# A hybrid attention and delta-rule block: gating and weight-tile work put in another order

## The chip, the cores and the metric

The kernel runs on one NeuronCore of a Trainium2 chip. The metric is the device time of one execution in microseconds (us), the median of several. The engines are TensorE (PE in the profile; PEld is its weight load), VectorE (DVE), ScalarE (ACT), GpSimd (POOL) and SyncE (SP, which here only issues DMA transfers and waits). They run side by side and meet at semaphores.

## The reference

One layer over a sequence of 1024 rows and 1024 channels, float32:

```python
mod = silu(c) @ ada_w + ada_b                     # shift, scale, gate
h = rms_norm(x, norm_g) * (1 + scale) + shift
p = h @ w_in                                      # 1024 x 6152, cut into twelve parts
o_sb = stick_breaking_attention(rms_norm(sb_q), rms_norm(sb_k), sb_v) * silu(sb_z)
q, k, v = split(silu(causal_conv4(dn_q | dn_k | dn_v)))
o_dn = gated_delta_rule(l2(q), l2(k), v, sigmoid(dn_b), decay(dn_a))
o_dn = rms_norm(o_dn, dn_norm_g) * silu(dn_z)
y = sigmoid(merge_sb) * (o_sb @ w_branch_sb) + sigmoid(merge_dn) * (o_dn @ w_branch_dn)
out = x + gate * (y @ w_out)
```

## The kernel before

Every large product is made in three passes: both operands are split into a high part (a cast) and a low part (the rest), and TensorE adds high x high, high x low and low x high in one PSUM bank. `project` (L839) does this for a tile of 128 output channels, one half of 512 rows at a time: 8 blocks of 128 inputs x 3 matmuls, 24 for a half tile.

**Weight tiles.** The list `tiles` holds, in order: tiles 0 and 1 of the gate columns (z of the attention), tiles 2 to 13 of the delta channels (T3 = 2), tiles 14 to 35 (the other z tiles and the two merge gates; T4 = 14), tiles 36 to 43 of the branch stage (T6 = 36), half from `w_branch_sb` and half from `w_branch_dn`. There is one raw buffer, `w3raw`, and two split ones, `w3hl`. For each tile `load_w3` (L815) waits until the low half of the tile before is written, then issues the DMA; `split_hi` (L821, VectorE) casts it, once TensorE has used the tile before the last; `split_lo` (L828, GpSimd) writes the low half; TensorE waits for both in `have_w3`. From the delta stage on the loads are issued by ScalarE (`copy_z`, piece 11 of 16 of a tile), the cast at piece 3 and the low half at piece 4 (`next_hi`, `next_lo`).

**The z pieces.** 24 tiles of z and merge gates don't belong to a stage: they fill TensorE where other work leaves it idle. One piece is one block of 128 inputs (3 matmuls), 16 are a tile, 8 a half tile. `z_piece` issues it into one of two banks; ScalarE copies a finished half tile (L923) and stores it to `z_scratch` (L887). TensorE may begin half tile m only when half tile m - 2 is copied.

**The order of the work**, written out by hand on each engine:

- `*_0`, `*_1`: norm, modulation, projection of q, k, v.
- `*_2`: attention in 64 steps (n = 0 to 63) and a few after. On TensorE each step has scores (L1054, L1056), `fill_2` (z pieces by the table `fill_at`), products with the values (L1085) and transposes of the weights (L1068); ScalarE makes sigmoids (L1132), copies transposed weights (L1140), the filled half (L914) and the outputs (L1149); VectorE scans (L1184). Split tile 1 lies in a buffer of its own; the second slot of `w3hl` lies under the attention's scan buffer `stick`.
- `*_3`: the twelve delta channels: projection, ScalarE's copy (L1283), four taps of the convolution on VectorE (L1303, L1306), silu. `dve_3` begins with `split_hi(T3 + 1)`, then the small decay chain `decays_in`, with help of ScalarE; before the second channel it casts tile 4.
- `*_4`: the delta rule over eight row blocks, with z pieces in between: `back_to_rows` (L1388), inverses, then a scan of eight steps (`from_state`, `solved`, `to_state`, `to_output`), `normalize_out` on VectorE and 32 closing transposes, `turn_output` (L1528), four to a block, which ScalarE copies (`copy_out_t`, L1661). The last z pieces ahead of these are those of half tile 41. SP's `sp_4` counts half tiles: in each turn m it waits for the copy of half tile m.
- `*_5`: the six half tiles 42 to 47 that are left (`left`) and the gates of eight tiles i, 0 to 3 from the attention, 4 to 7 from the delta rule: `silu_z` (L1914, ScalarE), `gated` (L1933, L1935, VectorE), `high_part` (L1918, ScalarE), `low_part` (L1940, VectorE). SP loads z and the attention's output for them in `load_gating` (L1904, L1906), two tiles a step, step 0 behind the end of `*_4` on all engines. The steps after those load the first half of `w_out` (L1909).
- `*_6`: the branch stage, eight tiles, two halves each. TensorE makes both branch products; ScalarE the sigmoid of the merge gates in `sg` (L1996); VectorE multiplies (L2015), GpSimd adds (L2034), VectorE casts the sum (`high`, L2005), GpSimd makes its low part (`low`, L2025). `high` and `low` of half n - 1 stand behind the product and the sum of half n. `split_w7` (L2045, L2047), the split of the first half of `w_out`, stands in this loop at n = 2 and 4. SP's `sp_6` issues the load of tile 37, then waits for all z stores, then loads `sg` (L1973).
- `*_7`: the output projection (L270 to L272), gate and residual.

Between the stages 1, 2 and 3 every engine but TensorE waits for the others (`end_phase`).

## Time and profile before

| what | us |
|---|---|
| median of 3 runs | 972.64 (972.01 to 973.81) |
| the profiled execution, its own time | 973.91 |
| its span, first to last instruction | 971.9 |
| TensorE busy / weight load | 939.9 / 789.2 |
| VectorE busy | 531.8 |
| ScalarE busy | 326.4 |
| GpSimd busy | 219.5 |

The share of each engine is an average over stages with different limits. The granted clock of TensorE is 1.00 (2.4 GHz) in nearly the whole span. TensorE's matmuls are pipelined, so those of one stream start 0.23 us apart though each is shown with 0.39 us. A row of the view in order of time ends with the idle time before it in brackets, and what released it as far as the semaphores show; "issue" means that the profile shows no releaser.

### The profile page before, as it was taken

To read this page: it belongs to the slowest core of one execution; us is meant where nothing else is said; L and a number is where in the kernel's file an instruction comes from. 1 tells how busy PE (TensorE), PEld (TensorE's weight loads), DVE (VectorE), ACT (ScalarE), POOL (GpSimd) and SP (SyncE) were. 2 spreads that over 40 slices of the span, in tenths; PEclk is the share of its full clock that TensorE was granted. 3 is DMA by queue.
4 is the path that set the end of the run, shared out by engine and by line. 5 is a ranking of instruction groups with operands and counts; after the bars stand their busy time and mean duration, and the time that the engine had idled before them with its cause. 6 is when DMAs were issued, how large, how long until landed. Compare 5 with 4: busy or idle time off the path is not lost.

```text
span 971.9 us, 13825 instructions
## 1 busy us (share of the span) xinstructions
PE 939.9 (97%) x5547; PEld 789.2 (81%) x5547; DVE 531.8 (55%) x769; ACT 326.4 (34%) x740; POOL 219.5 (23%) x130
## 2 busy tenths in 40 slices
PE   6899999999998899999999999999999999999998
PEld 6788889778887788888788888888887778787886
DVE  4967999688894445444044184133335548645322
ACT  7851222677785221212721110233223541110000
POOL 0003432610000111221343112101111117772000
PEclk9999999999999999999999999999999999999999
DMA  9943403511121221111223536311112873445321
GB/s 315 297 135 92 126 1 109 155 39 37 39 53 28 57 66 44 44 46 52 77 57 106 152 96 168 86 44 55 45 55 76 313 232 118 137 131 194 107 88 65
DMA packets 122697, 100.55 MB, mean 103 GB/s; under 512 B 18087, under 2 KB 104704, under 8 KB 122378
## 3 DMA queue, kind: packets, MB, share of 16 engines
q1 hardware_dynamic: 92330, 76.07, 26.2%
q10 hardware_dynamic: 30304, 23.60, 8.1%
q8 instruction: 44, 0.72, 0.3%
q14 instruction: 19, 0.16, 0.0%
HBM read 73.44 MB, written 24.12 MB: 100 GB/s over the span
## 4 chain that ended last, share of the span: by engine, by line
PE 66%; DVE 13%; DMA 8%; ACT 3%; POOL 3%; SPq 3%; issue 2%; ACTq 0%; POOLq 0%; DVEq 0%
PE psum L839 35%; PE psum L270 4%; PE psum L271 4%; PE psum L272 4%; DMA sg<-z_scratch 3%; PE psum L1068 3%; PE psum L1085 3%; DVE gacc L538 3%; DVE sq L714 2%; DMA adag<-in_ada_w 1%; PE psum L1420 1%; DVE stick L1184 1%; PE psum L1054 1%; PE psum L1056 1%; SPq L339 1%
## 5 line engine op out<-in xcount | busy, mean ns | idle before, releaser
L839 PE MATMUL psum<-hhi,w3hl 128*128 128x512 f32 x1120 | 365.8, 396 | 6.5 <-issue 4.7
L839 PEld LDWEIGHTS psum<-hhi,w3hl 128*128 128x128 f32 x1120 | 210.4, 188 | 51.3 <-issue 8.6
L839 PE MATMUL psum<-hlo,w3hl 128*128 128x512 f32 x560 | 218.2, 390 | 0.0
L828 POOL TENSOR_TENSOR w3hl<-w3raw,w3hl 128x1024 fp32r<-128x1024 f32 x43 | 102.7, 2389 | 470.2 <-DVE w3hl L821 452.9
L839 PEld LDWEIGHTS psum<-hlo,w3hl 128*128 128x128 f32 x560 | 105.4, 188 | 19.9
L1184 DVE TENSOR_TENSOR_SCAN stick<-stick,floor 128x1024 f32<-128x1024 f32 (+7 forms) x64 | 89.5, 1443 | 16.1 <-ACT stick L1132 15.5
L839 PE MATMUL psum<-ohi,w3hl 128*128 128x512 f32 x256 | 80.5, 394 | 3.1 <-issue 3.1
L821 DVE CAST w3hl<-w3raw 128x1024 fp32r<-128x1024 f32 x43 | 34.2, 796 | 73.3 <-DMA w3raw<-in_w_in 45.6
L923 ACT COPY zst<-psum 128x512 f32<-128x512 f32 x44 | 25.9, 589 | 131.1 <-PE psum L839 124.4
L674 PE MATMUL psum<-w,hhi 128*128 128x512 f32 x192 | 67.5, 396 | 0.0
L839 PEld LDWEIGHTS psum<-ohi,w3hl 128*128 128x128 f32 x256 | 48.9, 191 | 14.1 <-issue 3.9
L676 PE MATMUL psum<-w,hlo 128*128 128x256 f32 x192 | 53.8, 280 | 0.0
L839 PE MATMUL psum<-olo,w3hl 128*128 128x512 f32 x128 | 50.5, 395 | 0.0
L270 PE MATMUL psum<-w7hi,hhi 128*128 128x512 f32 x128 | 49.9, 390 | 0.6 <-POOL hlo L2025 0.6
L272 PE MATMUL psum<-w7hi,hlo 128*128 128x512 f32 x128 | 49.8, 389 | 0.0
L271 PE MATMUL psum<-w7lo,hhi 128*128 128x512 f32 x128 | 49.8, 389 | 0.0
L1068 PE MATMUL psum<-ident,stick 128*128 128x128 f32 x288 | 43.7, 279 | 3.6 <-ACT wTs L1140 2.6
L1306 DVE SCALAR_TENSOR_TENSOR cacc<-xpad,paramT,cacc 128x1024 f32<-128x1024 f32 x36 | 46.2, 1285 | 1.3
L270 PE MATMUL psum<-w,hhi 128*128 128x512 f32 (+1 forms) x128 | 44.4, 347 | 1.6 <-DVE hlo L501 0.9
L1283 ACT COPY xpad<-psum 128x512 f32<-128x512 f32 x24 | 14.0, 587 | 94.3 <-PE psum L839 94.3
L1132 ACT ACTIVATE stick<-psum 128x1024 f32<-128x1024 f32 (+7 forms) x64 | 42.7, 668 | 4.2 <-PE psum L1056 4.0
L271 PE MATMUL psum<-w,hhi 128*128 128x512 f32 (+1 forms) x128 | 43.4, 339 | 0.0
(234 smaller groups left out, 1593.2 us busy)
## 6 DMA issues: line engine op xcount, KB each, us to landing
z_scratch<-zst ACTq DMA_DIRECT2D x44, 256.0 KB, 2.2
w3raw<-in_w_in ACTq DMA_DIRECT2D x20, 512.0 KB, 4.2
ada<-in_ada_w SPq DMA_DIRECT2D x16, 512.0 KB, 7.6
w3raw<-in_w_in SPq DMA_DIRECT2D x16, 512.0 KB, 4.1
sg<-z_scratch SPq DMA_DIRECT2D x8, 1024.0 KB, 4.9
xrow<-in_x SPq DMA_DIRECT2D x4, 1024.0 KB, 6.1
w1raw<-in_w_in SPq DMA_DIRECT2D x4, 1024.0 KB, 7.1
adag<-in_ada_w SPq DMA_DIRECT2D x8, 512.0 KB, 4.0
```

The lines of the kernel that those rows point to most:

```text
L270: nc.tensor.matmul(out_, lh, rh, start=first, stop=False)
L271: nc.tensor.matmul(out_, lh, rl, start=False, stop=False)
L272: return nc.tensor.matmul(out_, ll, rh, start=False, stop=last)
L674: nc.tensor.matmul(bank(n % 4), h_hi, both_of(ch)[:, :, kt], start=kt == 0, stop=False, skip_group_check=True)
L676: t = nc.tensor.matmul(bank(n % 4)[:, 0:256], h_lo, high_of(ch)[:, kt, 0:256], start=False, stop=kt == KT - 1, skip_group_check=True)
L821: nc.vector.tensor_copy(weights(i)[0], w3raw[:]).then_inc(w3_hi, 1)
L828: nc.gpsimd.tensor_tensor(lo, w3raw[:], cast(hi), ALU.subtract).then_inc(w3_lo, 1)
L839: t = nc.tensor.matmul(out_, a[:, kt, :], moving[b][:, kt, 512 * half:512 * half + 512], start=(ends[0] and kt == k0 and m == 0), stop=(en ...
L1068: f = nc.tensor.transpose(t_cols(n, a)[:, P * (kb_ - 4 * a):P * (kb_ - 4 * a) + P], stick[:, n % NC, P * kb_:P * kb_ + P], ident[:, :])
L1132: nc.scalar.activation(stick[:, n % NC, 0:keys(n)], z_cols(n), ACT.Sigmoid, scale=-1.0).then_inc(keep_ok, 1)
L1184: nc.vector.tensor_tensor_scan(p_, p_, floor[:, S - keys(n):S][:, ::-1], 1.0, ALU.mult, ALU.max).then_inc(scan_ok, 1)
L1306: nc.vector.scalar_tensor_tensor(out=acc, in0=xpad[:, i % 2, k:k + S], scalar=tap[k], in1=acc, op0=ALU.mult, op1=ALU.add).then_inc(tap_ok, 1)
```

## The change

- Attention: the last two fill pieces of tile 1 are moved from steps 59 and 62 to step 65. Tile T3 + 1 = 3 is loaded by SP at step 56 and split at the attention's end on VectorE and GpSimd, no longer at the start of the projection.
- Delta projection: SP loads tiles 4 to 15 in it (before: 3 to 14, and 15 after its end).
- Gates: SP's loads of the gates begin two half tiles sooner, held by the semaphores of the work that last reads what they write over. Silus 0 to 3, gates 0 and 1 and high parts 0 and 1 are put into the end of `*_4` on ScalarE and VectorE. One z piece follows each four closing transposes. In `*_5` the order on ScalarE and VectorE is written anew: high parts 2 and 3 come ahead of the copy of half tile 42; the cast of tile 35 comes behind gates 6 and 7.
- Branch stage: `split_w7(0)` and `(1)` stand ahead of it. The first two loads of `sg` and the load of tile 37 are issued from `sp_4`. `high(n)` and `low(n)` follow the sum of their own half.

```diff
--- before.py
+++ after.py
@@ -887,8 +887,8 @@
             act.dma_start(half, staged).then_inc(z_out[m % 2], 16)
 
         FILL_BANK = 6
-        fill_at = {-1: 8, 0: 8}
-        fill_at.update({17 + 3 * j: 1 for j in range(PIECES)})
+        fill_at = {-1: 8, 0: 8, 65: 2}
+        fill_at.update({17 + 3 * j: 1 for j in range(PIECES - 2)})
 
         def fill_2(pe, step):
 
@@ -1011,6 +1011,8 @@
             for n in range(NST + 5):
                 if n == 2 * PER:
                     load_w3(sp, 2)
+                if n == 3 * PER + ST:
+                    load_w3(sp, T3 + 1)
                 u = turn_at(n)
                 if u is not None and u % 4 < 2:
                     second_half(u)
@@ -1199,6 +1201,7 @@
                     low(turn_at(n - 1))
                 if n in (13, 3 * PER):
                     split_hi(dve, 1 if n == 13 else 2)
+            split_hi(dve, T3 + 1)
 
         def pool_2(pool):
             nc.gpsimd.memset(cast(qk[HD:P, 0, 2]), 0.0).then_inc(c2_ok, 1)
@@ -1217,6 +1220,7 @@
             pool.wait_ge(q_mm, 8)
             split_lo(pool, 1)
             split_lo(pool, 2)
+            split_lo(pool, T3 + 1)
 
         names = ("tr sq y n uld vt va D dec G AT mout bin sub iout vin T32 c32 Y32 v32 X64 x64 T64 c64 Y64 v64 ktr kc KS R "
                  "QS qe Y xs xr SU S AV o so oy on OT aOT pre const bias cum e4 state")
@@ -1288,7 +1292,6 @@
 
         def dve_3(dve):
             nc.vector.memset(xpad[:, :, 0:TAPS - 1], 0.0).then_inc(tap_ok, 1)
-            split_hi(dve, T3 + 1)
             decays_in(dve)
             for i in range(CT):
                 if i >= 1:
@@ -1307,7 +1310,7 @@
                                                    op0=ALU.mult, op1=ALU.add).then_inc(tap_ok, 1)
 
         def pool_3(pool):
-            for i in range(1, CT + 1):
+            for i in range(2, CT + 1):
                 split_lo(pool, T3 + i)
 
 
@@ -1353,9 +1356,10 @@
 
                 return (BEFORE + at) // KT
 
-            load_w3(sp, fill_tile(F2 * PIECES) + 1)
             for m in range(2 * F2, 2 * NF):
-                load_gating(sp, m - AFTER)
+                load_gating(sp, m - (AFTER - AHEAD))
+                if m == 2 * NF - 1:
+                    load_w3(sp, T6 + 1)
                 sp.wait_ge(zc_ok, m + 1)
                 if m == half_tile(AT_MID + MID * ST // 2):
                     to_blocks(0)
@@ -1579,8 +1583,9 @@
             z(AT_TAIL, AT_TAIL + TAIL)
             for r in range(ST):
                 turn_output(r)
+                z_piece(pe, KT * AFTER + r)
             pe.drain().then_inc(phase_end, 1)
-            for n in range(KT * AFTER, NPIECES):
+            for n in range(KT * AFTER + ST, NPIECES):
                 z_piece(pe, n)
 
         def act_4(act):
@@ -1699,9 +1704,15 @@
                 squares_out(r)
                 z(at + 7, at + SCAN)
             rsqrt_out()
+            silu_z(act, 0)
+            silu_z(act, 1)
             z(AT_TAIL, AT_TAIL + TAIL)
             for r in range(ST):
                 copy_out_t(r)
+            for i in range(2):
+                high_part(act, i)
+            silu_z(act, 2)
+            silu_z(act, 3)
             act.drain().then_inc(phase_end, 1)
 
         def dve_4(dve):
@@ -1850,6 +1861,8 @@
                 z(at + 7, at + SCAN)
             normalize_out()
             z(AT_TAIL, AT_TAIL + TAIL)
+            for i in range(2):
+                gated(dve, i)
             dve.drain().then_inc(phase_end, 1)
 
         def pool_4(pool):
@@ -1881,23 +1894,28 @@
 
         z_in = [sem(f"z_in{i}") for i in range(ZT)]
         zs_silu, g_ok, ohi_ok, olo_ok = (sem("gz_" + n) for n in ("silu", "g_ok", "ohi", "olo"))
-
-        def left(one_half, gating):
-
-            for m in range(AFTER, 2 * NF):
-                for n in range(KT * m, KT * m + KT):
-                    one_half(n)
-                if m - AFTER < ZT:
-                    gating(2 * (m - AFTER))
-                    gating(2 * (m - AFTER) + 1)
+        AHEAD = 2
+
+        def left(one_half, a, b):
+
+            for n in range(KT * (AFTER + a), KT * (AFTER + b)):
+                one_half(n)
 
         def load_gating(sp, step):
             if step < 0:
                 return
             if step == 0:
-                sp.wait_ge(phase_end, 5 * 3 + 4)
+                sp.wait_ge(g["Y"], ST)
+                sp.wait_ge(g["KS"], ST)
+                sp.wait_ge(g["ktr"], ST)
                 for s_ in z_out:
                     sp.wait_ge(s_, 16 * 2 * ZT)
+            if step == ZT // 2:
+                sp.wait_ge(g["AV"], ST)
+            if step == ZT:
+                sp.wait_ge(phase_end, 5 * 3 + 4)
+            if step >= ZT + 2:
+                load_sg(sp, step - ZT - 2)
             for i in range(2 * step, 2 * step + 2) if step < ZT else ():
                 if i >= ZT:
                     sp.wait_ge(zs_silu, i - ZT + 1)
@@ -1908,47 +1926,56 @@
                 kts = slice(KT // 2 * (step - ZT), KT // 2 * (step - ZT + 1))
                 sp.dma_start(w7raw[0][:, kts], wout_v[:, kts, 0:512]).then_inc(w7_in[0], 16)
 
+        def silu_z(act, i):
+            act.wait_ge(z_in[i % ZT], 32 if i < ZT else 48)
+            nc.scalar.activation(zraw[:, i, :], zraw[:, i, :], ACT.Silu).then_inc(zs_silu, 1)
+
+        def high_part(act, i):
+            act.wait_ge(g_ok, i + 1)
+            nc.scalar.copy(ohi[:, i, :], zraw[:, i, :]).then_inc(ohi_ok, 1)
+
         def act_5(act):
-            def silu_z(i):
-                act.wait_ge(z_in[i % ZT], 32 if i < ZT else 48)
-                nc.scalar.activation(zraw[:, i, :], zraw[:, i, :], ACT.Silu).then_inc(zs_silu, 1)
-
-            def high_part(i):
-                act.wait_ge(g_ok, i + 1)
-                nc.scalar.copy(ohi[:, i, :], zraw[:, i, :]).then_inc(ohi_ok, 1)
-
-            def gate_act(i):
-                silu_z(i)
-                if i % 2:
-                    high_part(i - 1)
-                    high_part(i)
-
-            left(lambda n: copy_z(act, n), gate_act)
+            for i in (2, 3):
+                high_part(act, i)
+            for half in range(2):
+                left(lambda n: copy_z(act, n), half, half + 1)
+                for i in (ZT + 2 * half, ZT + 2 * half + 1):
+                    silu_z(act, i)
+                for i in (ZT + 2 * half, ZT + 2 * half + 1):
+                    high_part(act, i)
+            left(lambda n: copy_z(act, n), 2, 2 * NF - AFTER)
+
+        def gated(dve, i):
+            dve.wait_ge(zs_silu, i + 1)
+            v = zraw[:, i, :]
+            if i < ZT:
+                nc.vector.tensor_tensor(v, oraw[:, i, :], v, ALU.mult).then_inc(g_ok, 1)
+            else:
+                if i == ZT:
+                    dve.wait_ge(g["aOT"], ST)
+                nc.vector.scalar_tensor_tensor(out=v, in0=dnT[:, i - ZT, :], scalar=paramT[:, V_DG:V_DG + 1],
+                                               in1=v, op0=ALU.mult, op1=ALU.mult).then_inc(g_ok, 1)
 
         def dve_5(dve):
-            def gated(i):
-                dve.wait_ge(zs_silu, i + 1)
-                v = zraw[:, i, :]
-                if i < ZT:
-                    nc.vector.tensor_tensor(v, oraw[:, i, :], v, ALU.mult).then_inc(g_ok, 1)
-                else:
-                    nc.vector.scalar_tensor_tensor(out=v, in0=dnT[:, i - ZT, :], scalar=paramT[:, V_DG:V_DG + 1],
-                                                   in1=v, op0=ALU.mult, op1=ALU.mult).then_inc(g_ok, 1)
-
             def low_part(i):
                 dve.wait_ge(ohi_ok, i + 1)
                 nc.vector.tensor_tensor(olo[:, i, :], zraw[:, i, :], cast(ohi[:, i, :]), ALU.subtract).then_inc(olo_ok, 1)
 
-            def gate_dve(i):
-                gated(i)
-                if i % 2:
-                    low_part(i - 1)
-                    low_part(i)
-
-            left(lambda n: next_hi(dve, n), gate_dve)
+            left(lambda n: next_hi(dve, n), 0, 2)
+            for i in range(2, 2 * ZT, 2):
+                low_part(i - 2)
+                low_part(i - 1)
+                gated(dve, i)
+                gated(dve, i + 1)
+            left(lambda n: next_hi(dve, n), 2, 4)
+            low_part(2 * ZT - 2)
+            low_part(2 * ZT - 1)
+            left(lambda n: next_hi(dve, n), 4, 2 * NF - AFTER)
+            split_w7(dve, 0)
+            split_w7(dve, 1)
 
         def pool_5(pool):
-            left(lambda n: next_lo(pool, n), lambda i: None)
+            left(lambda n: next_lo(pool, n), 0, 2 * NF - AFTER)
 
 
         (y_hi, y_lo, w7_hi, w7_lo, f_mm, t_ok, res_ok) = (
@@ -1963,15 +1990,18 @@
 
             return bank((0 if i % 2 else 4) + 2 * branch + half)
 
+        def load_sg(sp, i):
+            for n in range(2):
+                sp.wait_ge(z_out[n], 16 * (2 * ZT + 2 * i + 2))
+            if i >= 2:
+                sp.wait_ge(y_lo, 2 * (i - 1))
+            sp.dma_start(sg[:, i % 2], z_dram[2 * ZT + 2 * i:2 * ZT + 2 * i + 2].rearrange("t p s -> p t s")
+                         ).then_inc(m_in[i % 2], 16)
+
         def sp_6(sp):
-            load_w3(sp, T6 + 1)
-            for n in range(2):
-                sp.wait_ge(z_out[n], 16 * NF)
             for i in range(KT):
                 if i >= 2:
-                    sp.wait_ge(y_lo, 2 * (i - 1))
-                sp.dma_start(sg[:, i % 2], z_dram[2 * ZT + 2 * i:2 * ZT + 2 * i + 2].rearrange("t p s -> p t s")
-                             ).then_inc(m_in[i % 2], 16)
+                    load_sg(sp, i)
                 if i + 2 < KT:
                     load_w3(sp, T6 + i + 2)
 
@@ -2013,11 +2043,7 @@
                 for branch in range(2):
                     v = sg[:, i % 2, branch, rows_of(half)]
                     nc.vector.tensor_tensor(v, v, br_bank(i, branch, half), ALU.mult).then_inc(tg_ok, 1)
-                if n >= 1:
-                    high(n - 1)
-                if n in (2, 4):
-                    split_w7(dve, n // 2 - 1)
-            high(2 * KT - 1)
+                high(n)
 
         def pool_6(pool):
             def low(n):
@@ -2032,9 +2058,7 @@
                 pool.wait_ge(tg_ok, 2 * n + 2)
                 a, b = (sg[:, i % 2, branch, rows_of(half)] for branch in range(2))
                 nc.gpsimd.tensor_tensor(a, a, b, ALU.add).then_inc(yt_ok, 1)
-                if n >= 1:
-                    low(n - 1)
-            low(2 * KT - 1)
+                low(n)
 
 
         def split_w7(dve, n):
@@ -2105,7 +2129,7 @@
             sp_2(sp)
             end_phase(sp, 2)
             sp.dma_start(c4raw[:], const_v[:, 5:8]).then_inc(g["const"], 16)
-            for i in range(1, CT + 1):
+            for i in range(2, CT + 2):
                 load_w3(sp, T3 + i)
             end_phase(sp, 3)
             sp_4(sp)
```

## Rows read from the trace of the kernel before

**Rows 1.** The page, busy time by engine.

```profile
PE 939.9 (97%) x5547; PEld 789.2 (81%) x5547; DVE 531.8 (55%) x769; ACT 326.4 (34%) x740; POOL 219.5 (23%) x130
```

**Rows 2.** In order of time, TensorE, the attention's end (start, us, engine, operation, idle before).

```profile
314.06 0.32 PE L1085 MATMUL psum<-wTs,rows 128*64 128x128 f32 x1 [1.54 <-ACT rows L1140]
```

**Rows 3.** In order of time, the projection of the delta channels.

```profile
327.26 0.47 PE L839 MATMUL psum<-hhi,w3hl 128*128 128x512 f32 x1 [0.89 <-POOL w3hl L828]
...
336.83 0.69 DVE L821 CAST w3hl<-w3raw 128x1024 fp32r<-128x1024 f32 x1
...
337.60 2.36 POOL L828 TENSOR_TENSOR w3hl<-w3raw,w3hl 128x1024 fp32r<-128x1024 f32 x1 [10.48 <-DVE w3hl L821]
...
340.05 0.47 PE L839 MATMUL psum<-hhi,w3hl 128*128 128x512 f32 x1 [1.66 <-issue]
```

**Rows 4.** In order of time, the delta stage's front; then its stretch, with the granted clock.

```profile
455.67 0.37 SPq L815 DMA_DIRECT2D w3raw<-in_w_in  x1
...
456.50 0.48 DVE L1811 MEMSET state<- 128x512 f32 x1
...
461.41 2.34 POOL L828 TENSOR_TENSOR w3hl<-w3raw,w3hl 128x1024 fp32r<-128x1024 f32 x1 [14.70 <-DVE w3hl L821]
...
463.85 0.47 PE L839 MATMUL psum<-hhi,w3hl 128*128 128x512 f32 x1 [1.86 <-issue]
...
core 0: us, PE busy (x) PEld busy (x) DVE busy (x) ACT busy (x) POOL busy (x), PEclk, DMA share, GB/s
460.00:475.00 15.00, 13.14 (x75) 10.93 (x75) 1.39 (x2) 9.57 (x65) 6.72 (x4) 1.00 0.25 73
```

**Rows 5.** In order of time, TensorE, the closing transposes.

```profile
747.61 1.03 PE L1528 MATMUL psum<-ident,dnT 128*128 128x128 f32 x8
749.52 1.11 PE L1528 MATMUL psum<-ident,dnT 128*128 128x128 f32 x8 [0.88 <-ACT dnT L1661]
750.91 1.12 PE L1528 MATMUL psum<-ident,dnT 128*128 128x128 f32 x8 [0.28 <-ACT dnT L1661]
...
753.72 0.47 PE L839 MATMUL psum<-hhi,w3hl 128*128 128x512 f32 x1 [0.29 <-POOL w3hl L828]
```

**Rows 6.** In order of time, ScalarE, the end of the delta rule.

```profile
734.21 0.59 ACT L923 COPY zst<-psum 128x512 f32<-128x512 f32 x1 [0.91 <-PE psum L839]
...
743.70 0.23 ACT L1656 ACTIVATE yo<-yo 128x32 f32<-128x32 f32 x1
```

**Rows 7.** Groups of instructions, 735 to 800 us (busy, mean ns | idle before).

```profile
L828 POOL TENSOR_TENSOR w3hl<-w3raw,w3hl 128x1024 fp32r<-128x1024 f32 x5 | 11.9, 2373 | 63.2 <-DVE w3hl L821 63.2
L1940 DVE TENSOR_TENSOR olo<-zraw,ohi 128x1024 fp32r<-128x1024 f32 x8 | 9.7, 1224 | 0.0
...
L1918 ACT CAST ohi<-zraw 128x1024 fp32r<-128x1024 f32 x8 | 8.4, 1053 | 3.5 <-DVE zraw L1935 2.6 <-DVE zraw L1933 0.5
L1914 ACT ACTIVATE zraw<-zraw 128x1024 f32<-128x1024 f32 x8 | 8.4, 1059 | 2.1 <-ACT zst L923 0.9 <-DMA zraw<-z_scratch 0.6 <-DMA oraw<-o_scratch 0.6
...
L1914 ACT ACT_TABLE_LOAD x1 | 1.3, 1283 | 0.4 <-ACT zst L923 0.4
```

**Rows 8.** In order of time, TensorE, four waits from the gates to the output projection.

```profile
776.61 0.47 PE L839 MATMUL psum<-hhi,w3hl 128*128 128x512 f32 x1 [0.88 <-issue]
...
790.09 0.47 PE L839 MATMUL psum<-ohi,w3hl 128*128 128x512 f32 x1 [2.32 <-issue]
...
836.25 0.47 PE L839 MATMUL psum<-ohi,w3hl 128*128 128x512 f32 x1 [0.78 <-issue]
...
885.41 0.47 PE L270 MATMUL psum<-w7hi,hhi 128*128 128x512 f32 x1 [0.61 <-POOL hlo L2025]
```

**Rows 9.** Busy time by stretch, columns as in rows 4.

```profile
791.07:794.48 3.41, 3.41 (x9) 2.63 (x8) 0.00 (x0) 0.00 (x0) 0.00 (x0) 0.50 1.03 305
```

**Rows 10.** DMA issues, 735 to 800 us (KB each, median us to landing).

```profile
sg<-z_scratch SPq DMA_DIRECT2D x2, 1024.0 KB, 7.8
w3raw<-in_w_in ACTq DMA_DIRECT2D x2, 512.0 KB, 4.6
```

## The prediction

> **What bounds the kernel now.** The busy times by engine come first: TensorE is busy for 97% of the span [rows 1]. So a gain can only come from the 32 us in which it is idle, and from any stretch at the lower clock; other engines' work counts only where it ends such a gap or makes one. The next view is TensorE in order of time, with its idle time and what ended it. About 7 us lie ahead of the first transpose and 4 us behind the last matmul; the change touches neither. The gaps that it can touch are these. At the attention's end TensorE waits 1.54 us for ScalarE [rows 2]. In the projection of the delta channels it waits 0.89 and 1.66 us, each time until GpSimd has written the low half of the next weight tile [rows 3]. The same wait of 1.86 us stands at the third block of the delta stage [rows 4]. Between the 32 closing transposes it waits 0.88 + 0.28 + 0.28 + 0.29 us for ScalarE's copies [rows 5]. Behind them it waits 0.88 us for tile 35, 2.32 us at the first branch matmul, 0.78 us in the branch stage and 0.61 us in the output projection [rows 8]. After the wait of 2.32 us the granted clock is 0.50, the 1.2 GHz level, for 3.41 us full of matmuls [rows 9]; that gives away half, 1.71 us.
>
> **Units.** From 790.09 to 836.25 there are eight half tiles of 24 matmuls; less 0.78 of wait and 1.71 of clock, one takes 5.46 us, and a piece of three matmuls 0.68 [rows 8, 9]. A silu or a high part takes ScalarE 1.06 us [rows 7], a copy of a half tile 0.59 [rows 6] (1.0 until the next operation, with the issue of its store behind it). A gate or a low part takes VectorE 1.22, and a low weight half takes GpSimd 2.37 [rows 7]. The cast ahead of that is 0.69 [rows 3].
>
> **Attention's end.** Two fill pieces, 1.36 us, move from steps 59 and 62 to step 65, into the 1.54 us hole. ScalarE's copy of the filled half moves behind the copies that TensorE waits for. Where the pieces leave, ScalarE's chain decides, so little of the 1.36 comes back there. Bounds: nothing, and the whole 1.54. I take 0.45, near the lower end, since the hole is filled rather than shortened.
>
> **Delta projection.** Tile 3 (T3+1) is loaded at step 56 and its cast waits only for the second filled half, a few us before the stage ends; cast and low half (3.1 us) end some 9 us before TensorE needs them. The 0.89 goes. VectorE no longer holds its decay chain behind this cast, so the first channel's taps start as soon as their input is there, some 5.5 us sooner, and the cast of tile 4 comes at about 331.4 instead of 336.83 [rows 3]. Its low half is done at 334.5, and TensorE needs it at 336.6. The 1.66 goes too. The load of tile 4 leaves earlier on SP's queue than before and has 12 us. Sum: 2.55.
>
> **Delta stage, front.** SP issues the load of tile 15 at 455.67, after everyone has ended the projection [rows 4]. With the change it goes in as soon as tile 14 is split, some 9 us before. The cast then follows VectorE's constants at about 457.0 [rows 4], the low half is ready at 460.1, and TensorE comes for it at 462. 1.86 goes. Nothing else waits on SP there.
>
> **Gates.** The transposes now alternate with pieces, so each round is 0.46 + 0.68 = 1.14 us, longer than a copy of ScalarE with its wait: the 1.73 us of waits go, and the eighth round ends at 747.61 + 9.1 = 756.7. The next tile would be wanted at 762.15. But high parts 0 and 1 and silus 2 and 3 stand behind the eighth copy, and *ahead of the copy of half tile 42*, whose bank TensorE needs at 762.15. The chain is serial: ScalarE's eighth copy ends 756.75, high part 0 at 757.8; VectorE low 0, low 1, gates 2 and 3 (four at 1.22) until 762.7; ScalarE high part 3 until 763.75 and the copy until 764.35. **A new wait of 2.3 us.** Then the copy's store, silu 4 until 765.85, silu 5 beside gate 4; gates 4 and 5 until 768.35, high part 5 until 769.45, copy of half tile 43 until 770.05, where TensorE came at 769.85: 0.25 us. Then silu 6 and 7 until 772.5, gates 6 and 7 until 774.05, and only behind them the cast of tile 35 and its low half: 774.75, 777.2. TensorE wanted it at 775.5: 1.75 us. The branch stage then starts at 777.3 + 2 x 5.46 = 788.2 in place of 790.09. Gain 1.9, not the 4.9 that the old waits add up to.
> Loads: SP issues those of gates 0 and 1 once half tile 39 is copied and the delta rule's last solve is through, about 735.2, and these 2 MB are there well before the first silu, which follows the scalar work that ends at 743.93 and the table load, at 745.2 [rows 6]. Tile 36 is loaded from about 777.3 behind half of w7 and the first merge tile; it has until 785 to land. A load of 512 KB took 4.6 us in this stretch, a merge tile of 1 MB 7.8 [rows 10]. Cost nothing, at most 0.5.
> The silu table is loaded (1.28 us, and the silu stands right behind it) ahead of ScalarE's tail of the z tiles instead of in the stretch behind it [rows 7]. Silu 1 ends at 747.3, before the copy that follows has its input. The Trainium skill (ScalarE: Activation LUTs, What ACT_TABLE_LOAD costs) counts another 1.38 us of drain for each switch; by it that copy would be late and the third transpose would wait some 0.3 us more, a sum of 9.55. The trace shows the load and no drain behind it, so I leave it out.
>
> **Clock.** TensorE reaches 790.09's place without the 2.32 us of idle, so 1.71 comes back. If the clock falls after the new 2.3 us wait, the two waits behind it take that up: ScalarE and VectorE set the time until 777.2, not TensorE.
>
> **Branch stage.** The two splits of w7's first half leave VectorE's branch loop and stand behind the cast of tile 36, done at about 792, and tile 37's cast follows them; its low half is there at 795, needed at 799. The 0.78 was such a split in the loop [rows 8]: it goes. The low part of y now follows its own sum in place of the next one. So the output projection's 0.61 goes, and the next merge tile is loaded earlier. VectorE waits for each sum of GpSimd now, 1.4 us of 5.46.
>
> **Sum:** 0.45 + 2.55 + 1.86 + 1.9 + 1.71 + 0.78 + 0.61 = 9.86. The profiled execution took 973.91, so 964.05; the median of the runs is 1.27 lower, so **962.8**.
>
> **Rivals.**
> *The clock falls after all* (0.12): the wait for tile 35 is 1.75 us. A gap of 1.86 left the clock at 1.00 [rows 4], one of 2.32 did not [rows 8, 9], so this is unlikely; there nothing takes it up. 964.5.
> *Tile 35 comes late* (0.12): ScalarE issues its load only at 768.4, behind the gates. If it takes the merge tile's 7.8 us [rows 10], it lands at 776.2 instead of before 774.05: 2.15 more, 965.0.
> *The gate chain is shorter* (0.11): ScalarE and VectorE overlap so that the waits of 2.3, 0.25 and 1.75 vanish. 962.8 - 4.3 = 958.5.
> *The weight waits only move* (0.06): the first three terms are given back, because the stage ends are held by the last attention stores, or tile 4 stays behind the taps. 967.7.
> *No change* (0.05): nearly all of it is given back.
> *Slower* (0.04): silu 0 and 1 stand ahead of ScalarE's last copies of the delta stage. If the gate loads land late, load of tile 34, copy of half tile 41, transposes and all behind them wait. They were issued at 735.2; each us past 745.2 costs one. The whole gain is gone if they land at 755, 20 us after the issue, where the merge tile took 7.8 [rows 10]. At 758 it gives 962.8 + 12.8 = 975.6.
>
> **Numbers.** The forecast has 0.50. The range, 960.2 to 967.0, takes in the attention's bounds, the clock, the late tile and half of the shorter chain. A measurement tells 0.2% here, 1.9 us: faster 0.91, same 0.05, slower 0.04.
>
> **What would show it.** No TensorE wait at the second and third projection tile and at the delta stage's third block; transposes without gaps; a wait of about 2.3 us near 757 to 760 on the new axis (762.2 less the 4.9 won ahead of it) ended by ScalarE's copy of half tile 42, and one of about 1.7 ended by GpSimd two half tiles later; clock 1.00 at the branch start; no gap in the branch stage. I am wrong if the stretch between the transposes and the branch stage has other gaps, or if weight loads land later than the casts want them.

## The result and the profile after

| what | before | after |
|---|---|---|
| median (4 runs each, side by side) | 972.33 (970.87 to 973.81) | **965.14** (963.96 to 965.26) |
| the profiled execution, its own time | 973.91 | 965.26 |
| its span | 971.9 | 963.3 |

The ratio is 0.9913, 95% interval 0.9899 to 0.9928 (the quotient of the two medians is 0.9926, inside it): faster by 7.2 us. A later series of six runs gave 965.0 and a ratio of 0.9914 [0.9894, 0.9934]. The forecast was 962.8 us: right in its range and sign, 2.3 us too hopeful. Two runs of the first series below, 2784.76 us of the kernel before and 1170.18 us of d1_front, lie far outside the others and are left out of its medians and ratios. The page, busy time by engine, then the chain that ended last, then one group (busy, mean ns | idle before):

```profile
PE 937.8 (97%) x5547; PEld 788.2 (82%) x5547; DVE 516.6 (54%) x769; ACT 325.9 (34%) x740; POOL 215.5 (22%) x130
...
PE 78%; DVE 13%; SPq 4%; DMA 2%; ACT 2%; issue 1%; POOLq 0%; DVEq 0%; ACTq 0%
...
L839 PE MATMUL psum<-hhi,w3hl 128*128 128x512 f32 x1120 | 368.6, 398 | 5.4 <-ACT zst L923 3.5
```

TensorE still bounds the kernel [rows 1]. Lines of the changed kernel are two higher in the attention and some twenty higher in the gates (L1940 is now L1962).

**Segments.** The front of the kernel shifts by up to 1 us from one execution to the next, so I cut the span at five TensorE rows and compare the pieces: first attention matmul of this view (170.06 us before, 170.64 after), first projection matmul (315.21, 314.45), first closing transpose (747.61, 741.67), first branch matmul (790.09, 785.06), first output projection matmul (879.88, 872.10), end.

| segment, us | before | after | gain | forecast |
|---|---|---|---|---|
| attention | 145.15 | 143.81 | 1.34 | 0.45 |
| projection to first transpose | 432.40 | 427.22 | 5.18 | 4.41 |
| transposes and gates | 42.48 | 43.39 | -0.91 | 1.9 |
| branch stage | 89.79 | 87.04 | 2.75 | 2.49 |
| output projection | 92.02 | 91.20 | 0.82 | 0.61 |
| sum | | | 9.18 | 9.86 |

The work ahead of the attention took 0.58 us longer in the execution profiled after, which leaves 8.60, the difference of the spans. Of the five terms one has the wrong sign. How firm that sign is stays open: a second profile of the changed kernel (after_again, below) has 41.96 for the transposes and gates, a gain of 0.52. Both are far from the 1.9 forecast. TensorE in order of time (start, us, operation, idle before in brackets), from the attention's end to the branch stage:

```profile
314.45 0.47 PE L839 MATMUL psum<-hhi,w3hl 128*128 128x512 f32 x1 [0.31 <-DVE w3hl L821]
...
760.21 0.47 PE L839 MATMUL psum<-hhi,w3hl 128*128 128x512 f32 x1 [3.54 <-ACT zst L923]
...
774.08 0.47 PE L839 MATMUL psum<-hhi,w3hl 128*128 128x512 f32 x1 [1.09 <-issue]
...
785.06 0.39 PE L839 MATMUL psum<-ohi,w3hl 128*128 128x512 f32 x1
```

The waits of [rows 3, 4] are gone, and the transposes run without the gaps of [rows 5]; the branch stage starts without one [rows 8]. The new wait is there, ended by ScalarE's copy as forecast, but with 3.54 us in place of 2.3. Now VectorE, then GpSimd, then ScalarE in the same stretch:

```profile
750.83 0.69 DVE L821 CAST w3hl<-w3raw 128x1024 fp32r<-128x1024 f32 x1 [4.25 <-DMA w3raw<-in_w_in]
751.77 4.46 DVE L1962 TENSOR_TENSOR olo<-zraw,ohi 128x1024 fp32r<-128x1024 f32 x2 [0.25 <-ACT ohi L1935]
...
758.47 2.36 DVE L1962 TENSOR_TENSOR olo<-zraw,ohi 128x1024 fp32r<-128x1024 f32 x2
...
769.92 0.69 DVE L821 CAST w3hl<-w3raw 128x1024 fp32r<-128x1024 f32 x1
770.52 4.54 DVE L1962 TENSOR_TENSOR olo<-zraw,ohi 128x1024 fp32r<-128x1024 f32 x2
```

```profile
751.60 2.41 POOL L828 TENSOR_TENSOR w3hl<-w3raw,w3hl 128x1024 fp32r<-128x1024 f32 x1 [15.37 <-DVE w3hl L821]
770.69 3.29 POOL L828 TENSOR_TENSOR w3hl<-w3raw,w3hl 128x1024 fp32r<-128x1024 f32 x1 [16.68 <-DVE w3hl L821]
```

```profile
740.03 0.39 ACTq L815 DMA_DIRECT2D w3raw<-in_w_in  x1
...
757.39 2.18 ACT L1935 CAST ohi<-zraw 128x1024 fp32r<-128x1024 f32 x2 [2.81 <-DVE zraw L1952]
759.48 0.58 ACT L923 COPY zst<-psum 128x512 f32<-128x512 f32 x1
```

Low parts 0 and 1 took 4.46 us, the same pair 2 and 3 took 2.36: the first pair lies over GpSimd's low half of tile 34, from 751.60 to 754.01. VectorE's pair ends 2.2 us behind that, just what the pair costs alone. So the two don't slow each other down a little; one stands still until the other's instruction is through. This is what the Trainium skill says (SBUF — State Buffer, SBUF: two separate sides): a VectorE operation with two inputs in SBUF and a GpSimd operation that reads SBUF need the same port pair under an exclusive lock, so whichever starts first has it for its whole instruction and the other blocks.

The profiles of the runs below agree. In these GpSimd began its low half of tile 34 first; the last column is how long it still ran when low part 0 began:

| profile | low parts 0 and 1, us | more than 2.36 | GpSimd still at work, us |
|---|---|---|---|
| after | 4.46 | 2.10 | 2.24 |
| after_again | 3.34 | 0.98 | 1.13 |
| e5_again | 2.84 | 0.48 | 0.63 |
| e7_loads_order | 2.75 | 0.39 | 0.53 |
| e5_load34, e6_order_load34, e8_order_only | 2.36 | 0 | 0 |

In e1_copy_first VectorE began first, 0.16 us ahead: there GpSimd took 3.32 us in place of 2.4, and the pair 4.57.

The kernel before has such a meeting too, which I overlooked when I priced every gate at 1.22: its gates 4 and 5, beside GpSimd's low half of tile 35, took 4.60 us where gates 6 and 7 took 2.48. VectorE, then GpSimd, before:

```profile
774.18 4.60 DVE L1935 SCALAR_TENSOR_TENSOR zraw<-dnT,paramT,zraw 128x1024 f32<-128x1024 f32 x2
...
782.02 2.48 DVE L1935 SCALAR_TENSOR_TENSOR zraw<-dnT,paramT,zraw 128x1024 f32<-128x1024 f32 x2 [0.89 <-ACT zraw L1914]
```

```profile
774.12 2.39 POOL L828 TENSOR_TENSOR w3hl<-w3raw,w3hl 128x1024 fp32r<-128x1024 f32 x1 [20.58 <-DVE w3hl L821]
```

In the changed kernel, behind the slow pair stand gates 2 and 3, high parts 2 and 3, and the copy of half tile 42 at 759.48. Tile 35 meets the same at 770.5: there GpSimd pays too, 3.29 in place of 2.37 [rows 7].

They meet since the load of tile 34, issued at 740.03, is there only at 750.8, 10.8 us later, where the one weight price that I had used was 4.6 [rows 10]. It also leaves late. On ScalarE it stands behind silus 0 and 1, which wait for the loads of gates 0 and 1; the last of these, issued by SP at 730.84, took 9.2 us and was there at 740.04, just when the weight load went out (DMA issues from 730.8 to 730.9 us):

```profile
oraw<-o_scratch SPq DMA_DIRECT2D x1, 512.0 KB, 9.2
```

The DMA issues from 738 to 757 us (KB each, us to landing) show it beside the gate loads that the change moved there; before, the load of that stretch took 4.2 us. First after, then before:

```profile
zraw<-z_scratch SPq DMA_DIRECT2D x3, 512.0 KB, 6.5
oraw<-o_scratch SPq DMA_DIRECT2D x2, 512.0 KB, 7.0
w3raw<-in_w_in ACTq DMA_DIRECT2D x1, 512.0 KB, 10.8
```

```profile
w3raw<-in_w_in ACTq DMA_DIRECT2D x1, 512.0 KB, 4.2
```

The clock, busy time by stretch (us, PE, PEld, DVE, ACT, POOL, granted clock, DMA share, GB/s):

```profile
741.67:785.06 43.39, 38.65 (x178) 31.12 (x176) 32.81 (x26) 21.99 (x28) 9.01 (x3) 0.96 0.72 241
785.06:872.10 87.04, 87.04 (x386) 72.10 (x384) 33.77 (x55) 17.11 (x10) 57.52 (x37) 1.00 0.39 122
756.67:760.21 3.54, 0.00 (x1) 0.04 (x1) 3.54 (x4) 2.58 (x3) 0.00 (x0) 1.00 0.00 0
761.50:764.50 3.00, 3.00 (x8) 2.31 (x7) 2.92 (x3) 2.44 (x4) 0.00 (x0) 0.50 0.92 354
```

It falls to 0.50 behind the new wait and costs nothing of its own: TensorE then waits 1.09 us for tile 35 instead of some 2.8.

**One time decides.** GpSimd ends tile 35's low half at 773.98, 32.3 us behind the first transpose; two half tiles later, 11.1 us, the branch stage starts at 43.4. The forecast had 29.6 and 40.6. Of the 2.7 us, the first collision explains 2.1 and the second 0.9; the rest of the chain ran 0.3 us shorter than forecast. The experiments are read by this time.

### The profile page after: what moved, and what is told of

Read it like the earlier page. It is cut to its first block, busy times and chain, and to the rows that moved or that the text cites. A ratio compares the mean times of both kernels' runs of the same rounds, so it can differ in the third digit from the quotient of the medians.

```text
span 963.3 us, 13833 instructions
## 1 busy us (share of the span) xinstructions
PE 937.8 (97%) x5547; PEld 788.2 (82%) x5547; DVE 516.6 (54%) x769; ACT 325.9 (34%) x740; POOL 215.5 (22%) x130
## 4 chain that ended last, share of the span: by engine, by line
PE 78%; DVE 13%; SPq 4%; DMA 2%; ACT 2%; issue 1%; POOLq 0%; DVEq 0%; ACTq 0%
PE psum L839 49%; PE psum L270 4%; PE psum L271 4%; PE psum L272 4%; DVE gacc L538 3%; PE psum L1070 3%; PE psum L1087 3%; DVE stick L1186 3%; SPq L339 2%; DVE sq L714 2%; PE psum L1424 1%; DVE ss L716 1%; SPq L343 1%; PE psum L1056 1%; PE psum L1058 1%
## 5 line engine op out<-in xcount | busy, mean ns | idle before, releaser
L828 POOL TENSOR_TENSOR w3hl<-w3raw,w3hl 128x1024 fp32r<-128x1024 f32 x43 | 104.7, 2436 | 461.8 <-DVE w3hl L821 461.8
L821 DVE CAST w3hl<-w3raw 128x1024 fp32r<-128x1024 f32 x43 | 29.5, 687 | 70.1 <-DMA w3raw<-in_w_in 49.3
L270 PE MATMUL psum<-w,hhi 128*128 128x512 f32 (+1 forms) x128 | 44.4, 347 | 1.8 <-DVE hlo L501 1.1
L1306 DVE TENSOR_SCALAR cacc<-xpad,paramT 128x1024 f32<-128x1024 f32 x12 | 9.0, 754 | 64.8 <-ACT xpad L1287 64.8
```

Of the source, the lines that this page charges most:

```text
L270: nc.tensor.matmul(out_, lh, rh, start=first, stop=False)
L821: nc.vector.tensor_copy(weights(i)[0], w3raw[:]).then_inc(w3_hi, 1)
L828: nc.gpsimd.tensor_tensor(lo, w3raw[:], cast(hi), ALU.subtract).then_inc(w3_lo, 1)
```

## The experiments

The kernel before ran beside every series: 973.97 us (median of 12 runs) in the first (d1_front, d3_turns, e1_copy_first, e4_pool_late), 972.19 (17) in the second (d2_branch, d5_front_branch, e5_load34, e6_order_load34), 974.04 (11) in the third (after_again, e5_again, e7_loads_order), 973.53 (7) in the last (e8_order_only). Ratios are to it, with their 95% intervals; they differ from the quotients of the medians by up to 0.0007. A segment comes from one profiled execution of each kernel.

### Where the gain lies: one part of the change at a time

**d1_front**: the kernel before with the hunks on `fill_at`, tile T3 + 1 and tile 15 alone:

```diff
-        fill_at = {-1: 8, 0: 8}
+        fill_at = {-1: 8, 0: 8, 65: 2}
...
+                if n == 3 * PER + ST:
+                    load_w3(sp, T3 + 1)
...
-            load_w3(sp, fill_tile(F2 * PIECES) + 1)
...
-            for i in range(1, CT + 1):
+            for i in range(2, CT + 2):
                 load_w3(sp, T3 + i)
```

> Of the change only the front: the two fill pieces at step 65, tile 3 loaded and split in the attention, tile 15 loaded in the projection. Theory (the weight waits are gone for good, and each removed wait is worth its idle time plus about 0.25 us of restart): the closing transposes begin 5.9 to 6.0 us sooner than before and the whole is 5.9 us shorter, since everything behind is bound by the same chain as before. Rival (part of the 5.9 us comes from the later parts of the change): under 5 us.

Measured: 965.91 us (3 runs), ratio 0.9921 [0.9898, 0.9944]. Segments: attention 143.29, projection to transposes 427.19, transposes and gates 42.05, branch 87.77, end 92.44. The first transpose comes 7.07 us sooner than in the profile before, where 5.9 to 6.0 was expected, and the run is some 8 us faster in place of 5.9. So nearly the whole gain of the change lies in the front. The wait at the branch start stays, yet the clock doesn't fall behind it:

```profile
782.59 0.47 PE L839 MATMUL psum<-ohi,w3hl 128*128 128x512 f32 x1 [2.37 <-issue]
```

**d3_turns**: the kernel before with the z pieces between the transposes alone:

```diff
                 turn_output(r)
+                z_piece(pe, KT * AFTER + r)
             pe.drain().then_inc(phase_end, 1)
-            for n in range(KT * AFTER, NPIECES):
+            for n in range(KT * AFTER + ST, NPIECES):
```

> Of the change only the z pieces between the closing transposes. Theory (the 2.5 us that TensorE wins there are lost again, because the gates begin only behind the transposes, which now end 3 us later, and the gate chain sets when tile 35 is there): within 1 us of before, with the wait for tile 35 grown from 0.9 to 3 us or more. Rival (TensorE sets the time there): 2.5 us faster.

Measured: 976.39 us (10 runs), ratio 1.0026 [1.0012, 1.0040]: slower by 2.4 us, where the theory allowed 1. The wait for tile 35 grew as expected. TensorE loses its gaps between the transposes and comes sooner to what ScalarE and VectorE have not finished; and these are later than before, since SP's gate loads wait for the end of the transposes and leave at 758.18 in place of 754.30, so that silus 0 and 1 wait 3.80 and 1.46 us for them:

```profile
770.55 0.50 PE L839 MATMUL psum<-hhi,w3hl 128*128 128x512 f32 x1 [1.39 <-ACT zst L923]
...
780.79 0.77 PE L839 MATMUL psum<-hhi,w3hl 128*128 128x512 f32 x1 [4.51 <-POOL w3hl L828]
```

The segment takes 45.59 in place of 42.48. Filling the gaps is worth nothing by itself here, as the stretch is set by the chain of gates.

**d2_branch**: the kernel before with `split_w7(0)` and `(1)` ahead of the branch stage and `high(n)`, `low(n)` behind the sum of their own half:

```diff
+            split_w7(dve, 0)
+            split_w7(dve, 1)
...
-                if n >= 1:
-                    high(n - 1)
-                if n in (2, 4):
-                    split_w7(dve, n // 2 - 1)
-            high(2 * KT - 1)
+                high(n)
```

> Of the change only the branch stage: high and low parts directly behind their own sum, the two splits of w7's first half ahead of the stage. Theory (two waits go, 0.78 and 0.61 us with 0.25 us of restart each, and the half clock at its start stays, since the wait ahead of it stays): 87.9 to 88.2 us from the first branch matmul to the output projection in place of 89.8, or 88.8 with the half clock in full, no gap in it, and 0.8 us less behind it; 1.8 us faster in all. Rival (the early splits delay tile 37): a new wait at the second branch tile, no gain.

Measured: 972.24 us (10 runs), ratio 0.9995 [0.9981, 1.0009]: no gain that can be told, where 1.8 us was expected. The waits of 0.78 and 0.61 us [rows 8] are gone, but one of 1.00 has come at the second branch tile, and the expectation's rival held. TensorE:

```profile
790.05 0.47 PE L839 MATMUL psum<-ohi,w3hl 128*128 128x512 f32 x1 [2.33 <-issue]
...
802.21 0.47 PE L839 MATMUL psum<-ohi,w3hl 128*128 128x512 f32 x1 [1.00 <-issue]
```

VectorE shows why:

```profile
792.03 1.23 DVE L2041 CAST w7hi<-w7raw 128x2048 fp32r<-128x2048 f32 x1 [4.61 <-DMA w7raw<-in_w_out]
...
798.96 0.69 DVE L821 CAST w3hl<-w3raw 128x1024 fp32r<-128x1024 f32 x1
```

Tile 37 is not late: SP issues its load at 789.91, as in the kernel before (789.95), which casts it at 794.92. But here the two splits of `w_out` stand ahead of that cast, and the first waits until 792.03 for loads that SP issued only from 780.45 to 786.45. In the changed kernel SP issues them at 765.66 and 771.60, both splits are done when tile 37 is cast at 788.86, and there is no such wait. So the branch edit needs the earlier load of `w_out`; that the two pay together is read from the rows, as no run has the loads alone.

**d5_front_branch**: the edits of d1_front and d2_branch together, so the change without its gates part and the earlier loads that go with it.

> The front and the branch order, with transposes, gates and their loads as before. Theory (the new order of gates and transposes is worth nothing, from the closing transposes to the branch stage it takes 43.4 us in place of 42.5): as fast as the changed kernel or up to 1.5 us faster, 963.5 to 965. Rival (the gates ahead of the delta rule's end do bring their part): 2 to 4 us slower than the changed kernel.

Measured: 965.70 us, just above the expected 963.5 to 965, ratio 0.9926 [0.9905, 0.9947], where the whole change has 0.9913 and 0.9914 in its two series. The gates part and its loads are worth nothing that shows.

### What limits the gates

**e1_copy_first**: the changed kernel, the copy of half tile 42 ahead of high parts 2 and 3.

```diff
         def act_5(act):
+            left(lambda n: copy_z(act, n), 0, 1)
             for i in (2, 3):
...
-                left(lambda n: copy_z(act, n), half, half + 1)
+                left(lambda n: copy_z(act, n), 1, half + 1)
```

> The changed kernel with ScalarE's copy of half tile 42 ahead of high parts 2 and 3. Theory (the chain of gates, not TensorE, sets when tile 35 is ready, and the copy with its store is 1.0 us of this chain): the wait of 3.5 us goes, two waits of about 2.5 us take its place (the copy of half tile 43, then tile 35), and the branch stage starts only 1.0 us sooner. Rival (the wait of 3.5 us is lost time by itself): 3.5 us faster.

Measured: 964.10 us, ratio 0.9900 [0.9879, 0.9922]; the segment 42.60, down 0.79. The branch stage starts sooner by nearly the 1.0 us expected. The wait went one half tile further back, where it is 3.07 us, and the one for tile 35 is 0.81 behind 3.4 us at half clock; two of about 2.5 were expected. The time by itself can't tell this from the changed kernel; the rows can.

**e4_pool_late**: GpSimd's split of tile 34 held until low parts 0 and 1 are written.

```diff
         def pool_5(pool):
+            pool.wait_ge(olo_ok, 2)
```

> The changed kernel with GpSimd's low half of tile 34 held until low parts 0 and 1 are written. Theory (VectorE and GpSimd slow each other when both read two tensors: the two low parts took 4.46 us in place of 2.4 because of this collision): they take 2.4 us, the wait at half tile 44 is about 1.5 in place of 3.5 us, and the branch stage starts 2.0 us sooner. Rival (low parts are slow from something else, transfers for one): they stay at 4.4 us, and TensorE waits 2 us longer for tile 34.

Measured: 965.16 us, ratio 0.9910 [0.9887, 0.9932]. VectorE's low parts 0 and 1 and gates 2 and 3, then GpSimd:

```profile
751.33 2.36 DVE L1962 TENSOR_TENSOR olo<-zraw,ohi 128x1024 fp32r<-128x1024 f32 x2 [3.25 <-ACT ohi L1935]
753.61 4.54 DVE L1952 TENSOR_TENSOR zraw<-oraw,zraw 128x1024 f32<-128x1024 f32 x2
```

```profile
753.77 3.30 POOL L828 TENSOR_TENSOR w3hl<-w3raw,w3hl 128x1024 fp32r<-128x1024 f32 x1 [17.98 <-DVE olo L1962]
```

Low parts 0 and 1 are back at 2.36 us, as expected. That alone doesn't show that GpSimd had doubled them: in this execution the load of tile 34 left at 737.37, so its cast stood ready at 748.07 and GpSimd would have been through before low part 0 even without the hold. What shows it is where GpSimd went: it now meets gates 2 and 3, which take 4.54 in place of 2.35. The extra time follows GpSimd's instruction. And the chain has gained nothing: the wait for half tile 42's bank is 3.63 where 1.5 was expected, the segment 46.10 where 2 us less than 43.39 was. (The profiled execution took 967.56 us, the median is 965.16.) The collision has to be taken out of the chain, not moved inside it.

**e5_load34**, and again as **e5_again** beside **after_again**, the changed kernel: the load of tile 34 issued ahead of the first silu, up to 2.2 us sooner.

```diff
             rsqrt_out()
+            load_w3(act, 34)
             silu_z(act, 0)
```

> The changed kernel with ScalarE issuing the load of tile 34 ahead of silu 0, so 2 us sooner and ahead of the loads of gates 2 and 3. Theory (the collision of GpSimd's low half with low parts 0 and 1 comes from this load's landing at 750.8, 10.8 us after its issue, behind 2 MB of gate loads): the cast follows gate 1 at once, GpSimd is through before low part 0, both low parts take 2.4 us, the wait at half tile 44 is about 1.5 us, and the branch stage starts 2 us sooner. Rival (the load lands late whatever its issue): no change.

> The changed kernel with only the load of weight tile 34 issued ahead of the first silu of z. Theory (that load was what made the two halves of tile 34 late and slow): 2.0 to 2.5 us faster than the changed kernel timed beside it, 962.5 to 963 us, since the stretch from the first closing transpose to the branch stage was 40.92 us against 43.39. Rival (the earlier gain came from comparing runs of two series): within 0.5 us of it.

> The changed kernel once more, as the measure for the two beside it: both theories give 964.5 to 965.5 us, as in its four runs so far.

First: 962.87 us (4 runs), ratio 0.9900 [0.9875, 0.9924]; the low parts at 2.36, segment 40.92, which is within 0.3 us of the 40.6 of the forecast that had no collision there. That looked like the cause found. Again, side by side: 965.57 (6 runs, ratio 0.9914 [0.9893, 0.9935]) against 965.0 for the changed kernel. **The rival held**: no gain can be measured, and the first figure doesn't repeat. The rows say why. Cast of tile 34 and low parts 0 and 1, first in e5_again, then in after_again:

```profile
751.52 0.69 DVE L821 CAST w3hl<-w3raw 128x1024 fp32r<-128x1024 f32 x1 [2.65 <-DMA w3raw<-in_w_in]
754.06 2.84 DVE L1963 TENSOR_TENSOR olo<-zraw,ohi 128x1024 fp32r<-128x1024 f32 x2 [1.85 <-ACT ohi L1936]
```

```profile
748.58 0.70 DVE L821 CAST w3hl<-w3raw 128x1024 fp32r<-128x1024 f32 x1 [3.14 <-DMA w3raw<-in_w_in]
750.64 3.34 DVE L1962 TENSOR_TENSOR olo<-zraw,ohi 128x1024 fp32r<-128x1024 f32 x2 [1.37 <-ACT ohi L1935]
```

Counted from the first closing transpose, the cast starts at 9.2 and 8.0 us in two executions of the changed kernel, at 6.8 and 7.6 with the load moved. What scatters is also the issue. Left where it was, the load went out 1.64, 2.92 and 1.68 us ahead of the first transpose (after, after_again, e1_copy_first), each time when gate 1's last load landed, but 3.87 and 3.86 us ahead in e4_pool_late and e8_order_only; moved, 3.87 or 3.88 in all four profiles. So in some executions the edit moves nothing. From issue to landing it took 9.8 to 11.4 us in all nine. The low parts take 4.46 and 3.34 without the move, 2.36 and 2.84 with it. The segment is 43.39 and 41.96 against 40.92 and 41.40: a difference that one or two profiles of each can't carry.

**e6_order_load34**: load 34 ahead; ScalarE's copies ahead of the high parts that they followed; the cast of tile 35 between low parts 2, 3 and gates 4, 5.

```diff
         def act_5(act):
+            for n in range(KT * AFTER, KT * AFTER + KT + 4):
+                copy_z(act, n)
             for i in (2, 3):
                 high_part(act, i)
...
+                if i == 4:
+                    left(lambda n: next_hi(dve, n), 2, 4)
                 gated(dve, i)
```

> The changed kernel with the load of tile 34 ahead of silu 0, ScalarE's copies of half tiles 42 to 44 and the loads of tiles 35 and 36 ahead of the high parts that they stood behind, and VectorE's cast of tile 35 ahead of gates 4 and 5. Theory (the gates are a chain that TensorE need not wait for; only the copies, loads and casts queued behind it held TensorE): no wait at half tiles 44 and 45, none for tile 35, and the branch stage starts 36.5 to 38 us behind the first closing transpose in place of 43.4; 5.5 to 7 us faster than the changed kernel, 958.5 to 960. Rival (high and low parts of tile 7 are the bound, or the tiles' loads land late under the gate loads): a wait of 2 us or more at the branch stage, 2 to 4 us faster.

Measured: 965.08 us, ratio 0.9924 [0.9905, 0.9942], segment 43.73: the expectation (958.5 to 960) missed. TensorE has one wait of 4.96 us, for a copy of ScalarE that ended at 773.19. VectorE, in order of time:

```profile
764.52 0.69 DVE L821 CAST w3hl<-w3raw 128x1024 fp32r<-128x1024 f32 x1 [4.02 <-DMA w3raw<-in_w_in]
765.13 4.61 DVE L1966 SCALAR_TENSOR_TENSOR zraw<-dnT,paramT,zraw 128x1024 f32<-128x1024 f32 x2
```

ScalarE issued that load at 756.56, behind copies that it now had first, and the cast stood 4.02 us in front of gates 4 and 5, which then met GpSimd. An early cast needs an early load.

**e7_loads_order**: e6_order_load34, but the load of tile 35 goes right behind high part 1, and the cast behind gates 4 and 5.

```diff
             for i in range(2):
                 high_part(act, i)
+            load_w3(act, 35)
             silu_z(act, 2)
...
                 gated(dve, i)
                 gated(dve, i + 1)
+                if i == 4:
+                    left(lambda n: next_hi(dve, n), 2, 4)
-            left(lambda n: next_hi(dve, n), 2, 4)
```

> Load of tile 34 ahead of the first silu, load of tile 35 right behind high part 1, ScalarE's copies of the half tiles ahead of the high parts that they used to follow, VectorE's cast of tile 35 behind gates 4 and 5. Theory (each remaining wait comes of an order or of a late load): GpSimd ends the low half of tile 35 some 25 us behind the first transpose, TensorE wants it at 25.4; no wait over 1 us in the gates stage; the branch stage starts 36.5 to 38 us behind the first closing transpose (43.4 in the changed kernel, 40.9 with the one load moved), so 5.5 to 6.5 us faster than the changed kernel, 958.5 to 960 us. Rival (the loads land late among the gate and z loads, or VectorE and GpSimd meet again): the stretch stays at 40 to 41 us and the time at 962 to 963 us.

Measured: **959.23 us** (958.17 to 959.75), ratio 0.9850 [0.9831, 0.9869]; the changed kernel beside it 965.0. The theory held: segment 36.59, no wait of 0.3 us or more in it.

**e8_order_only**: the same without the moved load of tile 34.

```diff
             rsqrt_out()
-            load_w3(act, 34)
             silu_z(act, 0)
```

> As the run with both loads moved and the copies ahead, but the load of tile 34 where the changed kernel has it, behind the first silu of z. Theory (what the moved load of tile 34 gave is too small to measure, as its second timing said; the order of the copies and the load of tile 35 carry the gain): the branch stage starts 36.5 to 38 us behind the first closing transpose, the ratio to the kernel before within 0.0015 of 0.985, so 958.5 to 960.5 us by a median of 974 of the kernel before. Rival (the load of tile 34 is what lets the rest come on time): the stretch at 39 to 41 us and the time back at 962 to 963.5 us, ratio 0.988 to 0.990.

Measured: 958.72 us (958.07 to 959.80), ratio 0.9852 [0.9835, 0.9868]. The order of ScalarE's copies and the place of tile 35's load and cast carry the gain, and no run separates these three from each other; tile 34's load adds nothing that shows. VectorE, GpSimd, then the two stretches:

```profile
761.12 0.69 DVE L821 CAST w3hl<-w3raw 128x1024 fp32r<-128x1024 f32 x1
761.72 2.35 DVE L1972 TENSOR_TENSOR olo<-zraw,ohi 128x1024 fp32r<-128x1024 f32 x2
763.99 4.61 DVE L1966 SCALAR_TENSOR_TENSOR zraw<-dnT,paramT,zraw 128x1024 f32<-128x1024 f32 x2
```

```profile
761.88 4.44 POOL L828 TENSOR_TENSOR w3hl<-w3raw,w3hl 128x1024 fp32r<-128x1024 f32 x1 [11.23 <-DVE w3hl L821]
```

```profile
741.25:777.89 36.64, 36.53 (x178) 30.14 (x176) 29.98 (x26) 21.68 (x28) 10.13 (x3) 1.00 0.82 281
777.89:864.93 87.04, 87.04 (x386) 72.07 (x384) 34.29 (x55) 17.11 (x10) 57.49 (x37) 1.00 0.40 122
```

VectorE and GpSimd still collide, and each loses 2 us, but GpSimd ends at 766.32, 25.1 us behind the first transpose in place of 32.3, and TensorE is busy for 36.53 of 36.64 us. It is the bound again, and this version is faster than both kernels: 6 us below the changed one by e7_loads_order's series, some 15 below the one before.

## Why the forecast was right, and where it was not

- **Waits removed in the front: right, each a quarter microsecond too small.** 0.89, 1.66 and 1.86 us add up to 4.41; the segment fell by 5.18, in d1_front by 5.21. The same holds behind it: the 0.61 gave 0.82, the 0.78 and the clock's 1.71 gave 2.75. The idle time of a row counts from the modelled end of the last matmul, so it leaves out some 0.25 us per stop: the last matmul is shown with 0.39 us though the next of a stream starts 0.23 behind it, and the first behind a stop takes 0.31 until the second starts.
- **Attention's end: mis-sized.** I took 0.45 of at most 1.54; it gave 1.34 in the profile, and 1.86 in d1_front. Profiles with this edit gave 143.3 to 144.3 us here apart from one of 145.70, in which the clock falls once; the profiles without it gave 145.15 and 145.33, and 145.75 with a fall. So the upper bound was the nearer one (0.25 us per stop puts d1_front above it): from 285 us to the first projection matmul TensorE's rows show 2.29 us of idle time before and 0.74 after, and no new wait stands where the pieces left, so ScalarE's chain was not the limit there that I took it for.
- **Gates: the step that failed.** "VectorE low 0, low 1, gates 2 and 3 (four at 1.22)" priced the low parts by rows in which GpSimd was silent [rows 7], though gates 4 and 5 of the same kernel stood beside it and took 4.60. The pair took 4.46. The cause stood in a cost that I had put at nothing: "A load of 512 KB took 4.6 us in this stretch". I used that for tile 36 and asked what the moved gate loads do to themselves, not what they do to tile 34's load, which puts GpSimd's split onto VectorE's chain. It is the last sign of being wrong that I had listed: a weight load landed later than its cast wanted it, by 4.25 us. The table of low parts and e4_pool_late show the collision by itself. The place of the new wait, its releaser and the second one at tile 35 were right; 1.9 of gain became -0.91 (0.52 in after_again).
- **Clock: right for this execution, but not by a rule that holds.** It fell behind the new wait, and the wait for tile 35 took it up. But the 1.71 us in the sum belongs to the profiled execution: the same wait of the kernel before is 2.33 us in d2_branch, with no fall behind it. And the chance of the clock rival rested on a gap of 1.86 us without a fall and one of 2.32 with one, as if the bound lay between: in d2_branch the clock fell behind the wait of 1.54 at the attention's end, which left it at 1.00 in the kernel before [rows 2].
- **Branch and output projection: right** in the whole change; alone (d2_branch) they give nothing, as the splits of `w_out` then wait for their load and hold up the cast of tile 37.
- **Rivals.** "The gate chain is shorter" did not happen here; e7_loads_order and e8_order_only are that case made on purpose. "Tile 35 comes late" was half right: late, not by its load but by its place behind gates 6 and 7. "Slower" was far off: the silus were in time, though gate 1's last load landed only just ahead of silu 1 and held back the load of tile 34 behind it.

That the load of tile 34 leaves with the landing of gate 1's load, and lands late beside the gate loads, is read from the traces; no run took those loads away, so how much each of them adds stays open.

## What to carry to other kernels

Price a moved operation by what runs beside it in its new place: a tensor operation of VectorE with two inputs in SBUF costs 1.2 us here and stands still while GpSimd does one of its own, so look for a place in the old profile where the two already meet, and ask of every load that lands late whose split it pushes onto whose chain. When a chain over several engines sets a stage, find the one time that decides (here the low half of the last tile) and put the cheap operations that other engines wait for, copies and load issues, ahead of the long ones; filling the bound engine's gaps gives nothing before that. And measure again before believing 2 us in 960.

## What the runs showed of the hardware

- VectorE and GpSimd block each other for whole instructions. The one that starts first keeps its time. Beside a GpSimd low half that ran first, VectorE's pair of 2.36 us became 2.75 to 4.46, by how long the two overlapped; GpSimd's 2.4 became 3.25 to 3.36 behind one VectorE instruction that had started, and 4.39 to 4.44 behind two. (Spans on GpSimd are rough; TensorE's waits that these low halves ended fit them.)
- It depends on what VectorE does. Two products with one operand in PSUM took 1.28 us beside GpSimd's low half, which took 2.40 (after, 790.77), as they do apart. A cast with its one input in SBUF held GpSimd: the low half took 3.31 behind the cast of `w_out` (after, 779.85 and 780.02).
- A 512 KB weight load took 4.2 us with no gate load beside it and 9.8 to 11.4 in nine profiles with 2 MB of gate loads issued around it.
- The clock after a wait is no sure thing. Behind 2.32 and 2.36 us (the kernel before, d5_front_branch) it fell to 0.50 for 3.41 us; behind 2.29, 2.31, 2.33 and 2.37 (e5_load34, e5_again, d2_branch, d1_front) it stayed at 1.00. It fell at the waits of 2.38 (after_again), 3.07 (e1_copy_first), 3.54, and 3.63 and 2.11 (e4_pool_late), but also behind 1.54 (d2_branch, 314.2 us) and 1.20 (e5_again, 214.2 us). In the two longest waits, 4.51 (d3_turns) and 4.96 (e6_order_load34), it fell some 2 us and more before their end and stayed at 0.50 for 6.8 us each. So the length of the wait doesn't decide alone, and a forecast can only give the fall a chance.
